# Compressed blocks from sums and differences of chunks, and prompt scores as two stacked float32r products

## The chip, the cores and the metric

The kernel runs on 1 core of one Trainium2 chip. The metric is the device time of one execution in microseconds (us), the median of the runs. Engines: PE (TensorE), DVE (VectorE), ACT (ScalarE), POOL (GpSimd), SP (SyncE, which issues DMAs here). Each runs its own program in order; they wait for each other through semaphores.

## The reference

One decoder layer for a prompt of 1024 tokens and 8 sample sequences of one new token over a paged cache of 2048. What matters here is one part of the sparse attention:

```
compress(rows, pos_emb, w1, w2):            # keys and values, 2 groups, head dim 64
    block n = rows 16 n .. 16 n + 31        # 32 rows, next block 16 rows on: two neighbours share a chunk of 16
    blk = (rows[block] + pos_emb).reshape(nb, groups, 32 * 64)
    return gelu(blk @ w1) @ w2              # w1: 2048 x 256, w2: 256 x 64
s = q . k / 8  over compressed keys, selected keys (top blocks) and the last 512 keys
p = masked softmax(s);  o = p . v  for each of the three, then gated and added
```

A block's product is `chunk c @ A + chunk c+1 @ B`, where A and B are the two halves of w1. The prompt has 63 blocks, each sample sequence 127. The prompt needs scores for 8 tiles of 128 tokens, 8 heads and three branches, with up to 1024 keys; all of it is f32, with a softmax behind it. Queries, keys and state are kept in f32; big weight products are done as three float32r products of a rounded part and a rest.

## The kernel before, in words

`build` runs stages one after the other, each a block with a program per engine; all engines meet between blocks.

`stage_project` (twice, to 458 us) normalises, projects and rotates; it leaves the turned (transposed) queries `qT` and keys `kselT`, `kwinT` in SBUF.

`stage_sequences` (458.7 to 940 us) compresses nine sequences (0 is the prompt, 1 to 8 the samples) and does the samples' attention. Its loop has eleven steps. Step s compresses the keys of sequence s (`compress(s, 0)`), then does the value product of sequence s-2 (`values`), the scores of s-1 (`scores`), and compresses the values of s (`compress(s, 1)`), with the block importance of s-1 between its quarters. The order is written by hand for each engine. In a `compress`, PE transposes the cached rows in four groups (L998, `turn_rows(0..3)`, two PSUM banks in turn), ACT copies each to `XT` (L1148, `keep_turned`), and PE multiplies: four quarters, each 4 row tiles of w1 by two halves of the 256 columns, 8 products with 254 moving columns (127 blocks, 2 groups; 126 for the prompt) in plain f32 (L1017). An f32 product shows as two MATMUL records. ACT applies the GELU straight from PSUM (L1157), and `compressed(q)` (L1035, L1040) multiplies by w2 at the start of the next keys' compress, before its first quarter. Under it, DVE copies turned keys (L1274), takes maxima (L1308, L1339), scales (L1289, L1292) and ranks the 30 blocks of a sequence by comparing all with all (L1327 to L1335); ACT copies scores (L1188) and does the exps (L1169, L1174, L1193). GELU and exp need different tables, each load shows as ACT_TABLE_LOAD. At the start of this stage DVE also gates the prompt's retention output (L1224 to L1233) and does the samples' retention step (L1238 to L1255), and PE computes the position bias (L957).

`stage_attention` (940.3 to 1310 us) goes through 192 units: 8 query tiles, 4 heads per group, 2 groups, 3 branches. For each unit: scores (L1471) with a mask added as a bf16 product (L1474), DVE maximum (L1567, L1570), ACT exp (L1517), PE transposes (L1488), copies by DVE or ACT (L1576, L1532), value products (L1500). A query has zeros in the other group's 64 partitions (`qz`, made by POOL in `pad_queries`), so that one f32 product with keys of both groups gives one group's scores; scores run three units ahead. Keys and queries lie in SBUF from the stages before; SP only loads `w_out`.

`stage_mix_out` and `stage_feed_forward` (to the end) multiply by w_out and do the SwiGLU; L374, L379 and L383 are the float32r product, rounding and rest, which all stages share.

## Time and profile before

| | |
|---|---|
| median of 3 runs | 2213.86 us (2211.0 to 2223.89) |
| the profiled execution | 2213.31 us, its span 2211.6 |
| PE, weight loads, DVE, ACT, POOL busy | 2095.4, 1812.5, 772.1, 599.4, 459.7 us |
| mean granted TensorE clock | 0.974 |
| L1017 (compress) | 1152 records |
| L1471 (prompt scores) | 720 records |
| L374 (float32r products) | 5184 and 1512 records |

In the rows below, a group of instructions is named by its line in the kernel, engine, operation, what it writes and reads, the shape, and the count. PE is the matmul, PEld the weight load that overlaps it. Brackets at the end of a row give how long the engine had been idle before it and what released it. A merged row of time covers all its instructions from the first start to the last end; the end of a matmul lies some 0.2 us after the next may start. The names arena, core, kept, halves, hidden are SBUF tensors, banks is PSUM.

### The profile page before, as it was taken

The page shows a single profiled execution, that of the slowest core. Times are in us where ns is not written, and L with a number is a line of the kernel's source. Part 1 is how long each engine was busy: PE and PEld are TensorE (multiplying, and loading weights), DVE is VectorE, ACT ScalarE, POOL GpSimd, SP SyncE. Part 2 cuts the span into 40 slices and gives each one's busy share as a digit, 9 for nine tenths or more (in the row PEclk, how much of TensorE's full clock was granted, in tenths as well). Part 3 has the DMA queues.
Part 4 walks back from the last instruction along what each step waited for, and adds up shares of the span by engine and source line. Part 5 has one row for each costly group of instructions (what it writes and reads, how often), then busy time and mean ns, then how long its engine had stood idle before and what let it go on. Part 6 is the DMA issues. An engine that isn't in the chain of part 4 may idle for free. (4 is left out here: it accounts for less than half of the span.)

```text
span 2211.6 us, 34591 instructions
## 1 busy us (share of the span) xinstructions
PE 2095.4 (95%) x12669; PEld 1812.5 (82%) x12669; DVE 772.1 (35%) x1454; ACT 599.4 (27%) x1269; POOL 459.7 (21%) x433
## 2 busy tenths in 40 slices
PE   6999989978999999699999989899999999999998
PEld 5777768856776777488888868699999999999987
DVE  5544433554344444455444453301111011111015
ACT  4310112112333333265444442222110111111112
POOL 0111112212223321210000002133321333223330
PEclk9999989988999999699999989999999999999999
DMA  5211102047886773020000002121111111111123
GB/s 176 68 58 39 39 26 84 30 103 123 112 108 103 100 100 52 24 68 1 1 1 1 1 29 106 66 75 43 45 48 47 48 47 43 43 51 44 45 69 116
DMA packets 159455, 131.89 MB, mean 60 GB/s; under 512 B 15257, under 2 KB 147050, under 8 KB 159010
## 3 DMA queue, kind: packets, MB, share of 16 engines
q1 hardware_dynamic: 155234, 121.85, 23.7%
q0 software_dynamic: 4096, 8.40, 2.2%
q8 instruction: 76, 1.25, 0.2%
q14 instruction: 49, 0.40, 0.1%
HBM read 117.85 MB, written 16.55 MB: 61 GB/s over the span
## 5 line engine op out<-in xcount | busy, mean ns | idle before, releaser
L374 PE MATMUL banks<-halves 128*128 128x344 f32 (+4 forms) x5184 | 855.8, 327 | 12.6 <-POOL halves L383 12.6
L374 PEld LDWEIGHTS banks<-halves 128*128 128x128 f32 (+1 forms) x5184 | 821.2, 188 | 43.1 <-issue 7.5
L383 POOL TENSOR_TENSOR halves<-core,halves 128x1024 fp32r<-128x1024 f32 (+1 forms) x143 | 243.8, 1712 | 641.4 <-ACT halves L379 491.4
L374 PE MATMUL banks<-hidden 128*128 128x512 f32 (+3 forms) x1512 | 349.7, 387 | 9.1 <-DVE hidden L383 9.1
L374 PEld LDWEIGHTS banks<-hidden 128*128 128x128 f32 (+1 forms) x1512 | 254.7, 179 | 77.6 <-issue 9.7
L1017 PE MATMUL banks<-arena 128*128 128x254 f32 (+1 forms) x1152 | 248.4, 372 | 11.2 <-ACT arena L1148 7.1
L1017 PEld LDWEIGHTS banks<-arena 128*128 128x128 f32 x1152 | 208.8, 194 | 37.4 <-issue 6.2
L379 ACT ACTIVATE halves<-core 128x1024 fp32r<-128x1024 f32 (+1 forms) x85 | 88.1, 1047 | 388.4 <-PE banks L374 369.6
L1929 DVE TENSOR_TENSOR core<-banks,core 128x344 f32<-128x344 f32 x66 | 34.0, 516 | 440.6 <-PE banks L374 440.6
L1500 PE MATMUL banks<-kept,arena 128*128 128x64 f32 (+1 forms) x1184 | 172.9, 277 | 6.4 <-ACT arena L1532 4.2
L1500 PEld LDWEIGHTS banks<-kept,arena 128*128 128x128 f32 (+1 forms) x1184 | 151.1, 191 | 20.6 <-issue 16.9
L1471 PE MATMUL banks<-kept,arena 128*128 128x128 f32 (+4 forms) x720 | 161.2, 342 | 0.9 <-PEq L849 0.9
L1517 ACT ACTIVATE arena<-banks,arena 128x63 f32<-128x63 f32 (+8 forms) x192 | 109.5, 571 | 166.9 <-DVE arena L1570 149.7
L1570 DVE TENSOR_REDUCE arena<-banks 128x1 f32<-128x640 f32 (+4 forms) x184 | 102.4, 558 | 128.1 <-PE banks L1474 126.4
L1471 PEld LDWEIGHTS banks<-kept,arena 128*128 128x128 f32 x720 | 116.6, 192 | 32.6 <-issue 16.2
L930 POOL DMA_DIRECT2D arena<-in_cache_kv x128 | 67.8, 530 | 235.4 <-PE banks L1058 209.7
L1488 PE MATMUL banks<-core,arena 128*128 128x128 f32 (+1 forms) x592 | 109.7, 280 | 0.2 <-ACT arena L1517 0.2
L561 POOL TENSOR_TENSOR retention<-core,retention 128x256 f32<-128x256 f32 (+1 forms) x36 | 30.3, 841 | 261.4 <-ACT core L544 261.4
L1576 DVE COPY arena<-banks 63x128 f32<-63x128 f32 (+4 forms) x129 | 59.5, 461 | 62.3 <-PE banks L1488 61.2
L1148 ACT ACTIVATE arena<-banks 128x512 f32<-128x512 f32 (+1 forms) x72 | 39.7, 577 | 147.5 <-PE banks L998 147.0
L629 DVE TENSOR_TENSOR retention<-core,retention 128x128 f32<-128x128 f32 (+1 forms) x72 | 37.6, 564 | 119.9 <-ACT core L544 119.9
L1880 ACT ACTIVATE core<-banks 128x344 f32<-128x344 f32 x66 | 30.2, 458 | 175.1 <-PE banks L374 175.0
(203 smaller groups left out, 1791.2 us busy)
## 6 DMA issues: line engine op xcount, KB each, us to landing
core<-in_cache_kv SPq DMA_DIRECT2D x128, 128.0 KB, 5.5
core<-in_w_gate SPq DMA_DIRECT2D x22, 512.0 KB, 3.8
core<-in_w_up SPq DMA_DIRECT2D x22, 512.0 KB, 3.7
core<-in_x_prompt SPq DMA_DIRECT2D x16, 512.0 KB, 3.4
arena<-in_cache_kv SPq DMA_DIRECT2D x128, 64.0 KB, 5.1
arena<-in_cache_kv POOLq DMA_DIRECT2D x128, 64.0 KB, 3.9
retention<-in_w_in SPq DMA_DIRECT2D x16, 448.0 KB, 6.2
...
```

Of the source, the lines that this page charges most:

```text
L374: done = pe.matmul(out, left[a], right[b], start=(first and i == 0), stop=(last and i == 2))
L379: return act.activation(hi, x, ACT.Copy)
L383: return engine.tensor_tensor(lo, x, hi.bitcast(F32), ALU.subtract)
L930: pool.dma_start(m.selv[16 * at:16 * at + 16, half, :, :], io.pool[bass.ds(page[pg], 1), :, :, 384:512].rearrange("a c t n -> (a c) t n")) ...
L1017: last = pe.matmul(m.banks[:, 2 + mt, 0:2 * nb], m.w1[kv][:, k, P * mt:P * mt + P], m.XT[:, k % 8, :, k // 8:k // 8 + nb], start=(k == 0), ...
L1148: act.activation(m.XT.rearrange("p (h j) g c -> p j h g c", h=2)[:, i, :, :, 0:nch], m.banks[:, u % 2, :].rearrange("p (g c h) -> p h g c" ...
L1471: last = pe.matmul(out[:, lo:hi], m.qz[t % 2][:, hh, g, :], keys[:, lo:hi], start=True, stop=not mask)
L1488: last = pe.transpose(m.banks[0:w, 5 + i % 2, P * x:P * x + P], m.prob[u % 4][:, P * (first + x):P * (first + x) + w], m.ident)
L1500: last = pe.matmul(m.banks[:, 7, HD * (u % 8):HD * (u % 8) + HD], m.pts[i % 3][0:w, P * x:P * x + P], v[0:w, 64 * g:64 * g + 64], start=(f ...
L1517: act.activation(m.prob[i % 4][:, 0:width(i)], scores_of(i, width(i)), ACT.Exp, bias=m.nmax[:, i % 8:i % 8 + 1], accum_out=m.sums[UNITS[i] ...
L1570: dve.tensor_reduce(peak, out, AX.X, ALU.max, negate=True).then_inc(s["c_max"], 1)
L1576: dve.tensor_copy(m.pts[i % 3][0:w, 0:P * n], m.banks[0:w, 5 + i % 2, 0:P * n]).then_inc(s["c_kept_dve"], 1)
```

## The change

- Compress: `m.odd` holds the odd chunks, `before` = even - odd of the same pair, `behind` = odd - next even. With A + B summed once per sequence set (`w1sum`), three products serve two neighbouring blocks: A on `before`, A + B on `odd`, B on `behind`. The block that starts at an even chunk is the first plus the second, the one that starts at an odd chunk is the second less the third. A quarter has 12 products of 128 moving columns (64 for the prompt) in place of 8 of 254. ACT copies only the odd chunks, DVE makes the differences out of PSUM and SBUF (`split`), ACT copies the shared product to SBUF (`keep_shared`), DVE forms the hidden rows (`summed`), and the GELU reads them from SBUF. `compressed` moves behind the first quarter. The pair `A + B` is added by DVE (keys) and POOL (values).
- The prompt's and samples' retention steps on DVE move in between the splits, sums and steps. Before, they came first.
- Blocks now stand in the order even, odd; masks and importance sums follow.
- Prompt scores: the stationary operand is the rounded part of a query tile on partitions 0 to 63 and its rest on 64 to 127, the moving one a group's keys, rounded, on both halves, and then their rest on both halves: two float32r products in place of one f32 product.
- For that, the project stage stores turned keys and queries to DRAM and waits for it; the sequences stage loads the keys at its end; the attention stage loads queries tile by tile, ACT rounds, POOL (queries) and DVE (keys) subtract, at its start and then a tile ahead. The bf16 masks are made in the sequences stage and kept.
- Semaphores of the project stage are cleared and freed behind it, with a barrier of all engines; SBUF is laid out anew.

The core of it:

```diff
+            def store_queries(t):
+                sp.dma_start(io.turned_queries[:, :, t * P:(t + 1) * P].rearrange("h p t -> p h t"),
+                             m.qT[:, :, t * P:(t + 1) * P]).then_inc(s["turned_out"], 16)
...
+                if ch in (5, 6) and t == 2:
+                    sp.wait_ge(s["tkept"], turns_before(n))
+                    sp.dma_start(io.turned_keys[ch - 5], (m.kselT, m.kwinT)[ch - 5]).then_inc(s["turned_out"], 16)
+                if kind == "q" and t >= 2:
+                    sp.wait_ge(s["tkept"], turns_before(n - 1))
+                    store_queries(t - 2)
...
+                sp.wait_ge(s["turned_out"], 16 * (2 + TP))
...
-                if kv == 0 and q:
-                    compressed(q - 1)
-                done = 2 * q + kv
-                if q == 0 and kv:
-                    pe.wait_ge(s["b_w_in1"], 48)
-                wait(pe, "b_gelu", 2 * done)
+                done, mc = 2 * q + kv, nch // 2
+                wait(pe, "b_summed", done)
                 for i in range(4):
                     if i in (1, 2):
                         turn_rows(i + 1)
-                    if done == 0 and i % 2 == 0:
-                        pe.wait_ge(s["b_w_in0" if i else "b_w_first"], 96 if i else 64)
-                    pe.wait_ge(s["b_kept_act"], kept_by(TURN_AT["kv"[kv], q, i] + 1, False))
-                    for k in (i, 4 + i, 8 + i, 12 + i):
+                    if q == 0 and (i == 0 or kv == 0 and i == 2):
+                        pe.wait_ge(s["b_w_sum"], 3 if kv else i // 2 + 1)
+                    pe.wait_ge(s["b_split"], kept_by(TURN_AT["kv"[kv], q, i] + 1, False))
+                    for j in (i, 4 + i):
                         for mt in range(2):
-                            last = pe.matmul(m.banks[:, 2 + mt, 0:2 * nb], m.w1[kv][:, k, P * mt:P * mt + P],
-                                             m.XT[:, k % 8, :, k // 8:k // 8 + nb], start=(k == 0), stop=(k == 15))
+                            for part, (w, x) in enumerate(((m.w1[kv][:, j, :], m.before), (m.w1sum[kv][:, j, :], m.odd),
+                                                           (m.w1[kv][:, 8 + j, :], m.behind))):
+                                bank, at = (3, P * mt) if part == 2 else (2, 256 * part + P * mt)
+                                out = m.banks[:, bank, at:at + P].rearrange("p (g c) -> p g c", g=2)[:, :, 0:mc]
+                                last = pe.matmul(out, w[:, P * mt:P * mt + P], x[:, j, :, 0:mc],
+                                                 start=(j == 0 and mt == 0 and part != 1), stop=(j == 7),
+                                                 skip_group_check=True)
+                    if i == 0 and kv == 0 and q:
+                        compressed(q - 1)
...
-                    act.activation(m.XT.rearrange("p (h j) g c -> p j h g c", h=2)[:, i, :, :, 0:nch],
-                                   m.banks[:, u % 2, :].rearrange("p (g c h) -> p h g c", g=2, h=2)[:, :, :, 0:nch],
-                                   ACT.Copy).then_inc(s["b_kept_act"], 1)
+                    act.activation(m.odd.rearrange("p (h j) g c -> p j h g c", h=2)[:, i, :, :, 0:mc],
+                                   turned_chunks(u, 1)[:, :, :, 0:mc], ACT.Copy).then_inc(s["b_kept_act"], 1)
+
+            def keep_shared(q, kv):
+                act.wait_ge(s["b_hidden"], 2 * q + kv + 1)
+                act.activation(products(m.shared, q), products(m.banks[:, 2, 256:512], q), ACT.Copy
+                               ).then_inc(s["b_shared"], 1)
...
+                act.wait_ge(s["b_summed"], 2 * q + kv + 1)
...
+                    keep_shared(step, 0)
...
+                    keep_shared(q, 1)
+                    if q + 1 in SEQS_B:
+                        keep_turned(q + 1, 0, range(2))
                     gelu(q, 1)
                     if q + 1 in SEQS_B:
-                        keep_turned(q + 1, 0)
+                        keep_turned(q + 1, 0, range(2, 4))
...
+            def split(q, kv, parts=range(4)):
+
+                mc = chunks_of(q) // 2
+                for i in parts:
+                    u = TURN_AT["kv"[kv], q, i]
+                    odd, before, behind = (x.rearrange("p (h j) g c -> p j h g c", h=2)[:, i, :, :, 0:mc]
+                                           for x in (m.odd, m.before, m.behind))
+                    even = turned_chunks(u, 0)[:, :, :, 0:mc]
+                    dve.wait_ge(s["b_kept_act"], kept_by(u + 1, False))
+                    dve.tensor_tensor(before, even, odd, ALU.subtract)
+                    dve.tensor_tensor(behind[:, :, :, 0:mc - 1], odd[:, :, :, 0:mc - 1], even[:, :, :, 1:mc], ALU.subtract
+                                      ).then_inc(s["b_split"], 1)
+
+            def summed(q, kv):
+
+                dve.wait_ge(s["b_shared"], 2 * q + kv + 1)
+                wait(dve, "b_gelu", 2 * (2 * q + kv))
+                shared = products(m.shared, q)
+                dve.tensor_tensor(products(m.hidden[:, 0, :], q), products(m.banks[:, 2, 0:256], q), shared, ALU.add)
+                dve.tensor_tensor(products(m.hidden[:, 1, :], q), shared, products(m.banks[:, 3, 0:256], q), ALU.subtract
+                                  ).then_inc(s["b_summed"], 1)
...
+            split(0, 0, range(2, 4))
+            norm_sums(0)
+            summed(0, 0)
+            split(0, 1)
+            norm_sums(1)
+            summed(0, 1)
+            split(1, 0, range(2))
+            norm_sums(2)
+            norm_sums(3)
+            split(1, 0, range(2, 4))
+            sample_out()
+            summed(1, 0)
+            split(1, 1)
+            sample_state()
+            summed(1, 1)
+            split(2, 0, range(2))
+            norm_gate(1, 1)
+            norm_gate(2, 2)
             dve.wait_ge(s["r_state_out"], 16)
...
                     dve.tensor_scalar(SR[:, WINC], SR[:, WINC], bst[:, 7:8], None, ALU.mult)
+                    if step in SEQS_B:
+                        split(step, 0, range(2, 4))
                     dve.wait_ge(s["b_sel_exp"], q)
                     inverse(bst[:, 6:7], m.gs[0:8, q - 1, 1:2], bst[:, 8:9])
                     dve.tensor_scalar(SR[:, SEL], SR[:, SEL], bst[:, 8:9], None, ALU.mult).then_inc(s["b_scaled"], 1)
+                    if step in SEQS_B:
+                        summed(step, 0)
...
                 q = step - 1
+                if step == 2:
+                    split(2, 0, range(2, 4))
+                    summed(2, 0)
...
                     dve.tensor_reduce(bst[:, 3:4], SR[:, WINC], AX.X, ALU.max, negate=True).then_inc(s["b_win_max"], 1)
+                    if step in SEQS_B:
+                        split(step, 1, range(2))
...
+                    if step in SEQS_B:
+                        split(step, 1, range(2, 3))
...
                     own.after(dve.tensor_tensor(cg, cg, ce, ALU.add))
+                    if step in SEQS_B:
+                        split(step, 1, range(3, 4))
                     own.after(dve.tensor_reduce(imp, cg, AX.X, ALU.add))
...
                     own.after(added)
+                    if step in SEQS_B:
+                        summed(step, 1)
+                    if step + 1 in SEQS_B:
+                        split(step + 1, 0, range(2))
                     dve.tensor_reduce(bst[:, 5:6], SR[:, SEL], AX.X, ALU.max, negate=True).then_inc(s["b_sel_max"], 1)
+                if step in (3, 4):
+                    norm_gate((0, 3)[step - 3], step)
...
+            def load_queries(t):
+
+                for g in range(2):
+                    src = io.turned_queries[:, HD * g:HD * g + HD, P * t:P * t + P].rearrange("h d t -> d h t")
+                    for half in range(2):
+                        sp.dma_start(m.qstage[t % 2][HD * half:HD * half + HD, g, :, :], src
+                                     ).then_inc(s[f"c_q_in{t % 2}"], 16)
+
+            for t in range(2):
+                load_queries(t)
...
+            sp.wait_ge(s["c_keys_lo"], 4)
...
-                        last = pe.matmul(out[:, lo:hi], m.qz[t % 2][:, hh, g, :], keys[:, lo:hi], start=True, stop=not mask)
+                        for v in range(2):
+                            last = pe.matmul(out[:, lo:hi], m.qs[t % 2][:, g, hh, :], pair[v][:, first + lo:first + hi],
+                                             start=(v == 0), stop=(v == 1 and not mask))
...
+            def queries_hi(t):
+
+                act.wait_ge(s[f"c_q_in{t % 2}"], 64 * (t // 2 + 1))
+                wait(act, "c_scores", PER_TILE * (t - 1))
+                round_to_hi(act, m.qs[t % 2], m.qstage[t % 2]).then_inc(s["c_q_hi"], 1)
+
+            queries_hi(0)
+            act.wait_ge(s["c_keys_in"], 128)
+            for g in range(2):
+                for what in range(2):
+                    round_to_hi(act, m.keys[what][g][0], m.kstage[what][g]).then_inc(s["c_keys_hi"], 1)
+            queries_hi(1)
...
+            def queries_lo(t):
+
+                pool.wait_ge(s["c_q_hi"], t + 1)
+                low = slice(HD, P)
+                rest_to_lo(pool, m.qs[t % 2][low], m.qstage[t % 2][low], m.qs[t % 2][low]).then_inc(s["c_queries"], 1)
+
+            queries_lo(0)
+            pool.wait_ge(s["c_queries"], 1)
+            queries_lo(1)
+            for t in range(TP - 1):
+                if t:
+                    pool.wait_ge(s["c_weighted"], t)
+                    queries_lo(t + 1)
+                pool.wait_ge(s["c_queries"], t + 2)
...
+            for g in range(2):
+                for what in range(2):
+                    dve.wait_ge(s["c_keys_hi"], 2 * g + what + 1)
+                    rest_to_lo(dve, m.keys[what][g][1], m.kstage[what][g], m.keys[what][g][0]).then_inc(s["c_keys_lo"], 1)
...
+            s.retire(PROJECT_ONLY)
```

## Rows read from the trace of the kernel before

**Rows 1.** Busy time of each engine in stretches: stretch, length, then busy (instructions).

```profile
618.00:666.00 48.00, 46.67 (x270) 36.26 (x268) 21.21 (x34) 17.61 (x31) 11.92 (x17) 1.00 0.73 103
...
1000.00:1100.00 100.00, 98.52 (x745) 85.06 (x744) 48.30 (x95) 50.55 (x150) 7.97 (x6) 1.00 0.01 1
```

**Rows 2.** Groups of PE by shape: prompt scores. Count, then busy us and mean ns.

```profile
L1471 PE MATMUL banks<-kept,arena 128*128 128x128 f32 x368 | 67.5, 276 | 0.0
L1471 PE MATMUL banks<-kept,arena 128*128 128x384 f32 x112 | 47.1, 502 | 0.0
...
L1471 PE MATMUL banks<-kept,arena 128*128 128x512 f32 x64 | 32.8, 594 | 0.0
...
L1471 PE MATMUL banks<-kept,arena 128*128 128x256 f32 x48 | 14.3, 380 | 0.0
```

**Rows 3.** Order of time, PE, sequences stage: start, length, line, shape, count.

```profile
471.25 3.73 PE L1017 MATMUL banks<-arena 128*128 128x126 f32 x32
...
718.46 1.09 PE L998 MATMUL banks<-core,arena 128*128 128x128 f32 x8
719.95 3.67 PE L1017 MATMUL banks<-arena 128*128 128x254 f32 x16 [0.40 <-ACT arena L1148]
...
724.73 0.38 PE L1100 MATMUL banks<-core,arena 8*8 8x127 f32 x2 [0.96 <-DVE core L1311]
...
753.91 1.47 PE L1049 MATMUL banks<-core,arena 8*128 8x8 f32 x21 [0.22 <-DVE arena L1292]
```

**Rows 4.** Order of time, PE, float32r at 512 and 256 columns, and the attention.

```profile
435.56 5.82 PE L374 MATMUL banks<-hidden 128*128 128x512 f32 x24
...
1182.10 1.00 PE L1500 MATMUL banks<-kept,arena 128*128 128x64 f32 x8
...
1183.94 1.68 PE L1471 MATMUL banks<-kept,arena 128*128 128x512 f32 x6
...
2157.89 5.20 PE L374 MATMUL banks<-halves 128*128 128x256 f32 x42
```

**Rows 5.** Weight loads of float32r (L374) and bf16 (L1474): ns min/median/max.

```profile
L374 PEld LDWEIGHTS banks<-halves x5184: 87/188/338, 1321.1 to 2197.2; 128*128 128x128 f32 x198, 128*8 128x8 f32 x2
...
L1474 PEld LDWEIGHTS banks<-arena x224: 100/100/154, 940.6 to 1302.3; 128*128 128x128 bf16 x112
```

**Rows 6.** Order of time, DVE: end of project, a step, start of attention.

```profile
456.56 0.67 DVE L652 TENSOR_SCALAR kept<-banks 128x512 f32<-128x512 f32 x1
...
734.44 2.27 DVE L1339 TENSOR_REDUCE core<-arena 8x1 f32<-8x2049 f32 x1
...
750.59 0.48 DVE L1289 TENSOR_SCALAR arena<-arena,core 8x512 f32<-8x512 f32 x1
...
940.93 0.22 DVE L1567 TENSOR_REDUCE arena<-banks 128x1 f32<-128x63 f32 x1 [0.95 <-PE banks L1474]
```

**Rows 7.** DMA issues of the page: KB each, us from issue to landing.

```profile
core<-in_w_gate SPq DMA_DIRECT2D x22, 512.0 KB, 3.8
```

**Rows 8.** Groups of DVE and ACT by shape: count, busy us, mean ns.

```profile
L663 DVE COPY retention<-banks 128x256 f32<-128x256 f32 x32 | 13.5, 423 | 5.4 <-PE banks L763 5.1
...
L379 ACT ACTIVATE halves<-core 128x1024 fp32r<-128x1024 f32 x84 | 87.9, 1056 | 388.4 <-PE banks L374 369.6 <-DMA core<-in_w_down 16.5 <-DMA core<-in_w_out 1.4
```

**Rows 9.** Order of time, ACT: the copy of a keys half's last transposes.

```profile
746.87 0.60 ACT L1148 ACTIVATE arena<-banks 128x512 f32<-128x512 f32 x1 [3.27 <-PE banks L998]
```

**Rows 10.** Order of time, PE: gaps and what follows them.

```profile
508.49 1.94 PE L998 MATMUL banks<-core,arena 128*128 128x128 f32 x8 [7.58 <-issue]
...
531.21 5.25 PE L1017 MATMUL banks<-arena 128*128 128x254 f32 x16 [2.62 <-ACT arena L1148]
...
564.72 1.03 PE L1071 MATMUL banks<-core,arena 128*128 128x128 f32 x8
...
891.68 2.41 PE L1049 MATMUL banks<-core,arena 8*128 8x8 f32 x21 [6.33 <-DVE arena L1292]
```

**Rows 11.** Busy time of each engine over the samples' retention step on DVE.

```profile
514.20:538.40 24.20, 21.58 (x103) 18.69 (x103) 23.80 (x13) 6.73 (x12) 5.84 (x1) 0.93 0.59 73
```

263 lines of the change are left out of this document (165 added, 98 removed).

## The prediction

> **What bounds the kernel now.** I read the windows by stage first [rows 1]. In a step of the sample sequences (618 to 666 us) the PE is busy 46.67 of 48 us, and in the attention of the prompt (1000 to 1100 us) 98.52 of 100, at a granted clock of 1.00; DVE and ACT are busy about half of the time or less. So the end is set by the stream of PE records, and a change pays only if it shortens that stream without making the PE wait for DVE or ACT. Then I read the PE groups by shape [rows 2] for the counts, and the order of time on each engine for pitches and for what each is late for. Mean durations don't serve, since records overlap: a pitch is the merged time less one lone record (0.27 to 0.38), over the count less one.
>
> All sums are against the profiled execution, 2213.3 us (span 2211.6), 0.6 under the median of the runs.
>
> **Pitches.** A plain f32 product is two records. At 254 columns 16 records take 3.67 us, 0.219 each; at 126 columns 32 take 3.73, 0.112 each [rows 3]: half the columns, half the time. At 64 columns eight take 1.00, 0.103 each [rows 4], so there the load of 128 weight columns sets the pace. For 128 columns I take 0.112. Scores in f32: 512, 256 and 128 columns, two records each, take 1.68 us [rows 4], so 0.84 ns a column: 0.431, 0.324, 0.216, 0.108 a record for 512, 384, 256, 128. A float32r product is one record, 0.237 at 512 columns (24 in 5.82) and 0.120 at 256 (42 in 5.20) [rows 4].
>
> **Prompt scores, in float32r.** The count of records stays: one product of two becomes two of one. From the counts in [rows 2], 64 records of 512 columns save 0.194 each, 12.4 us; 112 of 384 save 0.145 (the value between), 16.2; 48 of 256 save 0.096, 4.6. The 368 of 128 columns, and the compressed ones of 63, save nothing, being at the pace of the weight load. Sum 33.2 us, all on the PE's path. Bounds: 29 (a tenth lost to waits, since DVE's and ACT's part of a unit is unchanged) to 59 (rival D).
> By the Trainium skill, "TensorE: Matmul & The Clock Gate", the section on weight-path perf modes, a weight of 128 columns that is not FP32 is read in four parallel chunks. If float32r counts as not FP32, narrow score products get cheaper too, which is rival D. The trace speaks against it: a float32r LDWEIGHTS lasts 188 ns in the median, a bf16 one 100 [rows 5].
>
> **Start of the prompt stage.** Before, DVE's first maximum comes at 940.93 [rows 6], 0.6 after the stage begins. After, queries come back from DRAM: four loads issued over some 1.5 us, the last landing 3.8 later [rows 7]; then ACT rounds one query tile and four key tiles (5 x 1.06 [rows 8]) and DVE subtracts the last (about 1.1), all ahead of that maximum: 940.3 + 1.5 + 3.8 + 5.3 + 1.1 = 952.0. With a colder PE I take +11.5 (8 to 14). Later query tiles are loaded, rounded and subtracted a tile ahead of use: nothing.
>
> **Compressed blocks, the PE's share.** A quarter had 16 records of 254 columns and gets 24 of 128: 3.50 to 2.69 us. Over a step's eight quarters that is 6.5 us less. For sequence 0 it is a loss: 64 records at 0.112 become 96 at about 0.105, 2.9 more for keys and for values.
>
> **Compressed blocks, the chain.** What feeds a quarter was one ACT copy (0.60 for 512 columns [rows 9]). Now it is an ACT copy of 256 (0.39) and two DVE subtractions of 256 (0.42 each [rows 8], 0.75 for two that overlap a little), and where DVE does them is fixed by its program. I follow one cycle, from the values half of a step through the keys half of the next, 718.46 to 753.91 before [rows 3], with t = 0 at 718.46.
> - Quarter one started at 1.5 on ACT's copy; a split stands behind it now: 2.2 to 4.9. The importance product waits for ACT and DVE, 6.3 before [rows 3], less 0.4 of shorter copies: 5.9. Transposes 0.4, quarter two to 9.3, transposes, quarter three to 12.5.
> - DVE has 9.7 us of work from the importance product to the maximum of the selected scores (724.73 to 734.44 [rows 3, 6]). Two splits (1.5) and a wait for ACT's copy (0.3) go in between: 17.4. Split four is ready at 13.1, so quarter four ends at 15.8 and the next transposes at 16.7.
> - The sums out of PSUM (`summed`, 0.75) stand behind the ranking: 18.15; then the first split of the next keys: 18.9. **The PE waits 2.2 us**, where it waited for no DVE before.
> - Quarter 18.9 to 21.6, `compressed` 1.5, transposes, quarter two, transposes: 26.7.
> - `split(step, 0, range(2, 4))` stands on DVE behind the scaling of the window scores, their exp stands on ACT behind the copy of the last transposes, three small copies and a table load. In the trace this goes from 746.87 [rows 9] to 751.07, the end of that scaling [rows 6]: 4.2 us, less 0.2 for the shorter copy. So 26.85 + 4.0 + 0.75 = 31.6. **The PE waits 4.9 us** with nothing else to do.
> - Quarters three and four: 37.0, against 35.45 before; the rest of the cycle (13.8) is as it was.
> So a cycle of 49.2 gets 1.6 longer although the PE has 6.5 less to do; I take 1.8, for the cycles in which POOL's copies slow DVE. And gaps cost clock: after a gap of 2.62 us 16 records took 5.25 instead of 3.67 [rows 10, 3], and after one of 6.33 the next group 2.41 instead of 1.47, so part of it ran at the lower of the clock's levels (1.2, not 2.4 GHz). I take 1.6 once a cycle; 0 to 3.2 is possible. There are six such cycles, with the keys of steps 3 to 8: 6 x 3.4 = +20.4 (10 to 31). After step 8's values the PE waits for the maximum of the selected scores (6.33 [rows 10]), which comes 2.3 later, by two splits and the sums: +2.3.
>
> **Boundary and start of the sequences stage.** DVE's last copy of queries ends at 457.2 [rows 6]; their store must land before the stage ends, 3.8 later by the nearest row [rows 7]: 461.0 instead of 458.4. With issue and the new barrier 0.8 more: +3.4 (1.5 to 6). The sample retention moves in between the splits. Sequence 1's keys start at 508.49 [rows 10], when its pages are grouped; +3.4 and two more small loads in SP's queue, 1.1: 513.0. Transposes, copy and split 2.3, quarters 10.8, `compressed` 1.5, transposes 0.9: 528.5. DVE's retention was one piece of 24.2 us [rows 11], some 13.6 up to the sum of squares, which is `sample_out`: from 524.5 (after split four) to 538.1; sums and split 539.6. The PE waits 10, and runs the four quarters, the first cold, until 553.6. `sample_state`, the other 10.5, from 549.8: 560.3, sums and split 561.8, another 7 of waiting. A cold quarter 4.7, `compressed` 1.5, three quarters and transposes 9: 577.0, against 564.72 [rows 10]. That is +12.3, of which 3.4 is the boundary: +8.9 (4 to 14). Sequence 0's loss of 5.8 lies in front of the page wait (7.58 of idle PE [rows 10]), which hides it; without that wait it would count.
>
> **Sum.** 2213.3 + 3.4 + 8.9 + 20.4 + 2.3 + 11.5 - 33.2 = 2226.6. Feed-forward, output product and projections keep their work: 0.
>
> **Rivals.** A measurement of this kernel can tell about 0.5% (11 us) from no change.
> A (forecast): as above, 2227. Chance 0.40.
> B, the other side: **DVE keeps up**: quarter three is not held by the exp chain, nor the sums by the ranking. It decides at a PE wait under 0.5 us a cycle. Then the six cycles give -39 and the last nothing: 2213.3 + 3.4 + 8.9 - 39.0 + 11.5 - 33.2 = 2165. For it: DVE is busy only 21 of 48 us [rows 1]. Against: it is the order that makes the wait, not the load. Half true, it gives some 2195. Chance 0.20 for 2165 to 2202.
> C: the gaps are there but the clock holds, 6 x 1.8 in place of 6 x 3.4: 2217. For it: the gaps are short. Against: the row after 2.62 us. Chance 0.18.
> D: narrow float32r weights load fast. A 128-column record then costs half of a 256-column one and a fixed part, 0.066 in place of 0.112: 368 x 0.045, and with the compressed ones 26 us: 2201. Chance 0.07.
> E: both gaps of a cycle cost 1.6: 6 x 5.0: 2236; with the start at its upper bound 2245. Chance 0.15.
>
> The likeliest's own range is 2213 to 2240; 8 in 10 of all cases lie in 2188 to 2246. Under 2202.8 us: B and D, 0.27. Over 2224.9: E and seven tenths of A, 0.43. Between: 0.30.
>
> **What would show it.** Quarters of 24 records at 0.112. A PE gap of about 5 us before quarter three of each key half from step 3 on, ended by a DVE subtraction, and one of about 2 before quarter one; a cycle of 51 to 53 us. The prompt stage shorter by 22 us net, its first maximum 11 later than before, counted from the stage's start. If the gap before quarter three is missing, the chain through the window exp is wrong and B holds; if 128-column score records follow each other under 0.09 apart, D.

## The result, and the profile after

The changed kernel takes 2308.57 us (median of 4 runs, 2302.55 to 2309.52) against 2214.28 (4 runs): 1.0423 of the time before, 95% interval 1.0406 to 1.0440. The forecast was 2227 (2188 to 2246). The side was right, the size was not: +94 us where +13 was forecast. The profiled execution has a span of 2307.4 us and a mean granted clock of 0.929; before, 2211.6 and 0.974. One execution of e9 below, 2588.9 us at a granted clock of 0.743, is left out of its ratio.

From the page of the changed kernel, busy time of each engine over the span:

```profile
PE 2101.8 (91%) x13245; PEld 1876.2 (81%) x13245; DVE 851.8 (37%) x1645; ACT 607.1 (26%) x1299; POOL 465.2 (20%) x425
```

PE does 6 us more by this row, though many of its products got cheaper. The windows by stage say why. Columns as in [rows 1]; the number behind POOL's is the granted clock, 1.00 being 2.4 GHz ("warm" below) and 0.50 being 1.2 ("cold"):

```profile
471.00:491.00 20.00, 20.00 (x96) 20.00 (x96) 8.54 (x8) 0.56 (x2) 4.53 (x1) 0.50 0.50 116
...
504.00:524.00 20.00, 20.00 (x97) 20.00 (x96) 4.45 (x6) 0.56 (x2) 3.79 (x2) 0.50 0.86 160
...
1028.00:1131.00 103.00, 97.58 (x476) 92.28 (x477) 41.81 (x108) 44.00 (x158) 13.43 (x6) 0.50 0.21 52
...
1068.00:1108.00 40.00, 40.00 (x196) 38.15 (x196) 12.85 (x33) 15.39 (x56) 4.16 (x2) 0.50 0.05 14
...
1148.00:1188.00 40.00, 39.97 (x338) 38.50 (x338) 21.44 (x43) 23.56 (x70) 5.13 (x2) 1.00 0.05 15
```

Three stretches run at the lower level while PE is busy nearly all the time: the products of sequence 0's keys, those of its values (between them the products of the position bias bring the clock up, and a wait of 2.44 us follows), and the first 103 us of the prompt's attention. PE gets through 476 records in those 103 us and 338 in a later 40, so at the later rate the same records would need 56 us: less a wait of 4.42, some 42 us are lost there (the mix of shapes differs, so this is an estimate from those two rows). Before, the first 103 us of this stage had a mean granted clock of 0.98.

PE in order of time, changed kernel: start, length, line (L1065 the products of the compressed blocks, L1046 and L1125 transposes, L1103 and L1112 the values half, L1154 importance, L1635 scores of the prompt, L1653 its transposes, L1647 the last transposes of the mix), shape, count, idle time before and its releaser:

```profile
463.21 1.12 PE L1046 MATMUL banks<-core,arena 128*128 128x128 f32 x4 [4.76 <-POOL arena L990]
470.29 5.36 PE L1065 MATMUL banks<-arena 128*128 128x64 f32 x24 [5.96 <-DVE arena L1306]
...
534.31 1.09 PE L1046 MATMUL banks<-core,arena 128*128 128x128 f32 x8 [0.26 <-ACT arena L1181]
...
563.56 5.27 PE L1065 MATMUL banks<-arena 128*128 128x128 f32 x24 [12.89 <-DVE arena L1306]
...
585.05 4.79 PE L1065 MATMUL banks<-arena 128*128 128x128 f32 x24 [6.43 <-DVE arena L1306]
...
607.21 1.97 PE L1125 MATMUL banks<-core,arena 128*128 128x128 f32 x8 [6.82 <-DMA core<-out]
...
731.16 2.92 PE L1065 MATMUL banks<-arena 128*128 128x128 f32 x24 [1.11 <-DVE arena L1306]
...
743.93 2.94 PE L1065 MATMUL banks<-arena 128*128 128x128 f32 x24 [2.24 <-DVE arena L1306]
749.04 2.92 PE L1065 MATMUL banks<-arena 128*128 128x128 f32 x24 [1.29 <-DVE arena L1306]
...
761.94 7.78 PE L1065 MATMUL banks<-arena 128*128 128x128 f32 x48 [4.80 <-DVE arena L1306]
769.65 1.47 PE L1103 MATMUL banks<-core,arena 8*128 8x8 f32 x21
...
973.52 2.40 PE L1103 MATMUL banks<-core,arena 8*128 8x8 f32 x21 [6.34 <-DVE arena L1422]
...
1019.01 0.23 PE L1118 MATMUL banks<-core,arena 8*128 8x8 f32 x1 [0.37 <-DVE arena L1431]
1028.27 0.60 PE L1635 MATMUL banks<-kept_pairs,pairs 128*128 128x64 f32 x2 [9.03 <-POOL pairs L404]
...
1035.69 0.42 PE L1653 MATMUL banks<-core,softmax 128*64 128x128 f32 x1 [4.42 <-ACT softmax L1697]
...
1410.72 1.09 PE L1647 MATMUL banks<-core,softmax 128*128 128x128 f32 x4 [4.59 <-DVE softmax L1791]
```

Set against the same places of before ([rows 3, 10], and the first score and last mix at 940.46 and 1314.51), the 95.8 us of the span come from:

| stretch | before | after | more | forecast |
|---|---|---|---|---|
| up to the first transposes of the sequences | 459.76 | 463.21 | +3.5 | +3.4 |
| from there to sequence 1's scores | 104.96 | 144.00 | +39.0 | +8.9 |
| to the last transposing of probabilities | 326.96 | 366.31 | +39.4 | +22.7 |
| to the last product of the sequences | 47.92 | 45.72 | -2.2 | 0 |
| PE's wait for the first prompt score | 0.86 | 9.03 | +8.2 | } +11.5 |
| the prompt's attention | 374.05 | 382.45 | +8.4 | } -33.2 |
| the rest | 897.1 | 896.7 | -0.4 | 0 |

Within the prompt's attention each tile's mix is transposed once, so the starts of these transposes cut the stage into the same pieces of work in every trace. From the first score on, us:

| trace | first two pieces | third | other five |
|---|---|---|---|
| before | 57.7 | 37.2 | 279.1 |
| changed kernel | 98.6 | 35.3 | 248.6 |
| e3, f32 scores, hole in front | 70.3 | 37.2 | 279.2 |
| e2, f32 scores, the change's gaps | 76.2 | 37.2 | 279.1 |
| e1, float32r scores, gaps filled | 78.3 | 33.1 | 250.1 |
| e9, gaps filled, f32 scores in the first two tiles | 59.7 | 33.1 | 248.5 |

So the changed kernel gained 32.5 us on the score products in its last six pieces, and lost 40.9 in the first two.

### The profile page after: what moved, and what is told of

It is laid out like the page before. It is cut to its first block and busy times, and to the rows that moved or that the text cites. A ratio compares the mean times of both kernels' runs of the same rounds, so it can differ in the third digit from the quotient of the medians.

```text
span 2307.4 us, 36086 instructions
## 1 busy us (share of the span) xinstructions
PE 2101.8 (91%) x13245; PEld 1876.2 (81%) x13245; DVE 851.8 (37%) x1645; ACT 607.1 (26%) x1299; POOL 465.2 (20%) x425
## 5 line engine op out<-in xcount | busy, mean ns | idle before, releaser
L395 PE MATMUL banks<-halves 128*128 128x344 f32 (+4 forms) x5184 | 854.9, 327 | 13.1 <-POOL halves L404 13.1
L1065 PE MATMUL banks<-arena 128*128 128x128 f32 (+1 forms) x1728 | 245.8, 310 | 88.6 <-DVE arena L1306 88.6
L1065 PEld LDWEIGHTS banks<-arena 128*128 128x128 f32 x1728 | 238.3, 224 | 95.2 <-DVE arena L1306 44.0
L1665 PE MATMUL banks<-kept,softmax 128*128 128x64 f32 (+1 forms) x1184 | 191.3, 297 | 6.1 <-ACT softmax L1712 4.3
L1665 PEld LDWEIGHTS banks<-kept,softmax 128*128 128x128 f32 (+1 forms) x1184 | 169.6, 211 | 15.9 <-issue 8.4
L1697 ACT ACTIVATE softmax<-banks,softmax 128x64 f32<-128x64 f32 (+8 forms) x192 | 109.4, 571 | 144.4 <-DVE softmax L1762 135.6
L1762 DVE TENSOR_REDUCE softmax<-banks 128x1 f32<-128x640 f32 (+4 forms) x184 | 102.4, 558 | 116.1 <-PE banks L1639 115.3
L1653 PE MATMUL banks<-core,softmax 128*128 128x128 f32 (+1 forms) x592 | 120.6, 301 | 4.4 <-ACT softmax L1697 4.4
L1635 PE MATMUL banks<-pairs 128*128 128x128 f32 (+3 forms) x592 | 123.0, 338 | 0.7 <-DVE pairs L404 0.7
L1635 PEld LDWEIGHTS banks<-pairs 128*128 128x128 f32 x592 | 105.8, 222 | 3.6 <-issue 1.0
L1653 PEld LDWEIGHTS banks<-core,softmax 128*128 128x128 f32 (+1 forms) x592 | 80.3, 167 | 9.3 <-ACT softmax L1697 4.6
L1768 DVE COPY softmax<-banks 64x128 f32<-64x128 f32 (+4 forms) x129 | 59.4, 460 | 75.3 <-PE banks L1653 74.8
```

The source lines that it names most:

```text
L395: done = pe.matmul(out, left[a], right[b], start=(first and i == 0), stop=(last and i == 2))
L1065: last = pe.matmul(out, w[:, P * mt:P * mt + P], x[:, j, :, 0:mc], start=(j == 0 and mt == 0 and part != 1), stop=(j == 7), skip_group_che ...
L1635: last = pe.matmul(out[:, lo:hi], m.qs[t % 2][:, g, hh, :], pair[v][:, first + lo:first + hi], start=(v == 0), stop=(v == 1 and not mask))
L1653: last = pe.transpose(m.banks[0:w, 5 + i % 2, P * x:P * x + P], m.prob[u % 4][:, P * (first + x):P * (first + x) + w], m.ident)
L1665: last = pe.matmul(m.banks[:, 7, HD * (u % 8):HD * (u % 8) + HD], m.pts[i % 3][0:w, P * x:P * x + P], v[0:w, 64 * g:64 * g + 64], start=(f ...
L1697: act.activation(m.prob[i % 4][:, 0:width(i)], scores_of(i, width(i)), ACT.Exp, bias=m.nmax[:, i % 8:i % 8 + 1], accum_out=m.sums[UNITS[i] ...
```

## The experiments

Ratios are to the kernel before, run on the same chip; us in brackets are medians. A gain over the changed kernel is the difference of two medians taken on different chips; from the ratios it comes out 1 to 3 us smaller. Line numbers in rows of an experiment are those of its own kernel.

**e1. The prompt stage's gaps filled.** On PE, ahead of the first score and behind the third:

```diff
+FILL_A, FILL_B = 10, 5
...
+            def fill(count):
+                for _ in range(count):
+                    pe.matmul(m.banks[:, 6, :], m.ident, m.vsel[:, 0:4, :], start=True, stop=True)
+
+            fill(FILL_A)
...
+                if x == AHEAD:
+                    fill(FILL_B)
```

> The changed kernel, with 10 extra 128x512 f32 products of resident data in front of the prompt attention's first score product and 5 more behind its third unit, into a bank that nothing has read from yet: PE has no idle 9.03 and 4.42 us there any more. Theory (the gap lets the clock fall to the 1.2 GHz level, and the small float32r, transposing and value products behind it don't bring it up for 100 us; once up, they hold it): the stretch 1028 to 1131 us runs at the granted clock 1.00 from its start, which is worth about 103 us x (1 - 196/338 records in equal 40 us slices) = 43 us: 2308 - 43 = 2265, at least 2255 to 2275. Rival (the mix of small products cannot hold the high level for the first two tiles, whatever stands in front): the clock falls again within some 20 us of the first score, and the time stays at 2300 to 2310. Rival 2 (the start is set by the waits on the queries and key parts, not by the clock): 2305 to 2312.

Measured 1.0346, 1.0329 to 1.0364 (2289.57): 19 us gained, between the two forecasts. Windows of its trace, with the wait at which the clock fell:

```profile
1028.00:1048.00 20.00, 18.15 (x124) 13.63 (x123) 15.22 (x40) 12.40 (x51) 3.59 (x2) 1.00 0.58 151
...
1060.17 0.98 PE L1673 MATMUL banks<-kept,softmax 128*128 128x64 f32 x4 [1.13 <-DVE softmax L1776]
...
1059.00:1062.00 3.00, 1.87 (x12) 1.86 (x11) 2.19 (x6) 1.30 (x5) 1.16 (x1) 0.71 0.06 16
1062.00:1100.00 38.00, 38.00 (x187) 36.38 (x187) 11.77 (x32) 15.30 (x52) 1.29 (x1) 0.50 0.05 13
```

The stage starts at 1.00 now, and loses it after some 30 us, right behind a wait of 1.13 us at the end of the first tile; it stays low for 41 us, PE busy throughout. The kernel before has the same wait and the same fall, and is back within 4 us:

```profile
966.35 0.63 PE L1500 MATMUL banks<-kept,arena 128*128 128x64 f32 x4 [0.99 <-DVE arena L1576]
...
968.00:971.00 3.00, 3.00 (x14) 2.54 (x14) 0.43 (x1) 0.75 (x3) 0.00 (x0) 0.50 0.00 0
971.00:974.00 3.00, 3.00 (x29) 2.89 (x26) 1.52 (x5) 2.14 (x9) 0.00 (x0) 0.95 0.00 0
```

So neither theory holds alone. At this place, behind a wait of 1.0 to 1.6 us, the clock falls with either kind of score product (before, e1, e9, e11 and e12; not in e6). How long it stays down differs: 41 us here, with float32r scores behind it, and under 4 in the other four, with f32 ones.

**e2. The same gaps, f32 scores.**

```diff
-                        for v in range(2):
-                            last = pe.matmul(out[:, lo:hi], m.qs[t % 2][:, g, hh, :], pair[v][:, first + lo:first + hi],
-                                             start=(v == 0), stop=(v == 1 and not mask))
+                        last = pe.matmul(out[:, lo:hi], m.qs[t % 2][:, g, hh, :].bitcast(F32),
+                                         pair[0][:, first + lo:first + hi].bitcast(F32), start=True, stop=not mask)
```

> The changed kernel, with each prompt score product done once, as plain f32 on the rounded part of the keys, in place of two float32r products; the low part of the keys drops out of the scores. All staging, waits and the two gaps at the stage's start stay. Theory (it is the two cheap float32r products that leave the array too little to do for the clock to rise): the clock comes back to 1.00 within some 20 us of the stage's start, as the kernel before had it from 945 us on, and the stage costs about what it did before, 374 us, plus the two gaps: 1.0 to 1.05 of the kernel before's, 2308 - 10 = 2298 give or take 6, with the low-clock stretch gone. Rival (a stage that starts cold stays cold for 100 us whatever its score products are): the low clock lasts as long, the f32 products are dearer, and the time is 2320 to 2350.

Measured 1.0477, 1.0459 to 1.0494 (2318.55). Windows of its trace:

```profile
1028.00:1048.00 20.00, 14.93 (x70) 12.55 (x70) 12.29 (x28) 8.88 (x34) 3.10 (x1) 0.50 0.62 156
1048.00:1068.00 20.00, 20.00 (x97) 17.77 (x96) 7.22 (x28) 8.91 (x39) 0.00 (x0) 0.50 0.29 56
1068.00:1088.00 20.00, 19.61 (x163) 17.82 (x162) 10.62 (x28) 12.72 (x47) 5.12 (x2) 0.96 0.10 27
```

The low stretch is 40 us, not 103: with f32 scores the clock comes back 60 us sooner, behind the same two gaps (9.14 and 4.33 here). The time is still 10 us above the changed kernel, since the wide scores cost their old price again (33 us by the forecast's count). My 2298 reckoned with a return within 20 us.

**e3. The kernel before, with a hole** ahead of the first prompt score.

```diff
             pe.wait_ge(s["c_masks"], 4)
+            pe.wait_ge(s["hole"], 1)
...
             own = Links(dve, s, "own_dve")
+            for _ in range(7):
+                own.after(dve.tensor_tensor(m.prob[3], m.vsel.rearrange("p t n -> p (t n)"),
+                                            m.vwin.rearrange("p t n -> p (t n)"), ALU.add))
+            dve.tensor_tensor(m.prob[3], m.vsel.rearrange("p t n -> p (t n)"), m.vwin.rearrange("p t n -> p (t n)"),
+                              ALU.add).then_inc(s["hole"], 1)
```

> The kernel before, with its first prompt score product held back by eight 128x1024 additions on DVE of about 1.1 us each, so that PE idles about 9 us where it idled 0.86 us. Theory A (f32 products bring the clock back soon): 2214 + 8 to 9 for the hole + up to 10 for a cold start = 2222 to 2233. Rival (any hole there costs a long stretch at the 1.2 GHz level): 2214 + 9 + about 40 = 2255 to 2270. If both this and the f32 scores in the changed kernel come out short, the hole is only half of the cause and the lighter products the other half.

Measured 1.0107, 1.009 to 1.0124 (2236.16), 22.5 us more, 3 above the range of theory A and far from the rival. PE's first score, and windows of its trace:

```profile
950.40 0.66 PE L1472 MATMUL banks<-kept,arena 128*128 128x63 f32 x2 [10.86 <-DVE arena L1562]
```

```profile
950.00:960.00 10.00, 9.60 (x47) 8.54 (x48) 4.10 (x17) 4.55 (x21) 0.00 (x0) 0.50 0.49 170
...
970.00:990.00 20.00, 19.77 (x114) 17.57 (x112) 9.18 (x28) 9.13 (x37) 3.99 (x3) 0.63 0.01 1
990.00:1010.00 20.00, 19.39 (x166) 17.84 (x167) 9.63 (x29) 12.54 (x48) 1.22 (x2) 1.00 0.00 1
```

10.0 us are the hole (10.86 less 0.86), 12 to 13 the cold stretch of some 35 us behind it. So a hole there costs its length and as much again with f32 scores. With the float32r ones the cold stretch costs some 42 us by the rates above, and 37 set against the same pieces of e9 (41.1 more in the first three, less the wait of 4.42).

**e4. Sequence 0 over 128 columns**, the upper half zeros.

```diff
-                done, mc = 2 * q + kv, nch // 2
+                done, mc = 2 * q + kv, 64
...
+            for x in (m.odd, m.before):
+                own.after(dve.memset(x[:, :, :, 32:64], 0.0))
```

> The changed kernel, with sequence 0's compressing products taken over 128 columns in place of 64 (the other 64 are zeros from a memset and their results are not read). The products count stays at 384 records. At the high clock a 128-column record took 0.115 us and at the low one 0.22; a 64-column one was seen at 0.22 only. Theory (narrow products, limited by the weight load, leave the array idle enough that the clock stays at the 1.2 GHz level): the clock rises within the first 10 us, sequence 0 takes about 2 x (4 x 2.8 + a few) us less, sequence 1's keys start 15 to 22 us earlier, 2287 to 2295. Rival (the clock stays low there because PE comes cold out of the gap before it, whatever the width): 2306 to 2312, with 0.22 us a record still. Rival 2 (the 64-column record costs 0.22 at either clock): the clock may rise in the wide run, which then also saves, so the other run of narrow products behind a fill has to tell it.

Measured 1.0354, 1.0337 to 1.0371 (2291.81): 17 us gained by doing twice the columns. PE of its trace, both halves of sequence 0:

```profile
469.13 4.37 PE L1065 MATMUL banks<-arena 128*128 128x128 f32 x24 [5.97 <-DVE arena L1306]
473.55 2.84 PE L1065 MATMUL banks<-arena 128*128 128x128 f32 x24
...
493.10 4.33 PE L1065 MATMUL banks<-arena 128*128 128x128 f32 x24 [2.44 <-DVE arena L1306]
```

Out of the same gaps, the clock is up within the first quarter of 24 records.

**e8. Sequence 0 with 64 columns, the gap ahead of it filled.**

```diff
                 turn_rows(1)
+                if q == 0 and kv == 0:
+                    for _ in range(7):
+                        pe.matmul(m.banks[:, 7, :], m.ident, m.vsel[:, 0:4, :], start=True, stop=True)
```

> The changed kernel, with seven 128x512 f32 products of resident data in PE's 5.96 us wait ahead of sequence 0's first compressing product; the compressing products keep their 64 columns. Theory (64-column products cannot hold the high clock): if the clock is up at their start it falls again within 10 to 15 us, most records cost 0.22 us still and the time is 2300 to 2309. Rival 1 (it was the cold start alone; once up, 64-column products hold the clock): 0.11 us a record, sequence 1 starts some 20 us earlier, 2286 to 2293 as with 128 columns. Rival 2 (a 64-column record costs 0.22 at the high clock too): the windows show a granted clock near 1.00 with 0.22 us a record.

Measured 1.04, 1.0379 to 1.0421 (2300.3). PE of its trace, keys and then values of sequence 0:

```profile
471.65 2.79 PE L1068 MATMUL banks<-arena 128*128 128x64 f32 x24
...
493.94 5.29 PE L1068 MATMUL banks<-arena 128*128 128x64 f32 x24 [2.44 <-DVE arena L1309]
499.45 5.22 PE L1068 MATMUL banks<-arena 128*128 128x64 f32 x24
504.89 10.34 PE L1068 MATMUL banks<-arena 128*128 128x64 f32 x48
```

It split in two. Entered at the high clock, a 64-column record costs 0.116 us and the level holds for that half. Behind the bias products and a 2.44 us gap, the same products ran 21 us at 0.22 without bringing it back; e4's, behind the same gap, did. So here they kept a clock they found, for 11 us, and did not raise it in 21. Rival 2 (0.22 at either clock) is out.

**e5. The float32r scores alone**, compressing and retention as before. Of the change, all of `stage_attention`, the stores and loads of queries and keys and `kcbP` stay; in `stage_sequences` the products are again:

```diff
-                    for j in (i, 4 + i):
+                    for k in (i, 4 + i, 8 + i, 12 + i):
...
+                            last = pe.matmul(m.banks[:, 2 + mt, 0:2 * nb], m.w1[kv][:, k, P * mt:P * mt + P],
+                                             m.XT[:, k % 8, :, k // 8:k // 8 + nb], start=(k == 0), stop=(k == 15))
```

> One half of the change alone: the two stacked float32r score products with all their staging (queries and keys out to DRAM and back, rounded and low parts), while the compressing keeps the four products, the copies and the retention work of the kernel before. Theory (the clock is the cost of this half): +3.4 for the boundary, +12.6 for the two gaps at the prompt stage's start, -39 for the score products at the high clock, +43 for the 100 us at the 1.2 GHz level = 2214 + 20 = 2234, 2228 to 2242; so this half alone is slower, and the sequences' part of the loss (some 75 us) belongs to the compressing. Rival (the scores pay, all of the loss is in the sequences): 2185 to 2200. Rival 2 (the staging of keys also delays the sequences, for instance the transfer that scores of sequence 1 waited for): 2250 or more.

Measured 1.0075, 1.0047 to 1.0104 (2228.92), as expected. Its sequences end at 941.7, 2.1 later than before (rival 2 is out); its attention takes 16 us more, with the same low stretch as the changed kernel:

```profile
951.00:1051.00 100.00, 94.85 (x463) 89.53 (x463) 40.79 (x106) 42.91 (x156) 13.31 (x5) 0.50 0.21 53
```

So of the 94 us some 17 belong to the scores and 77 to the compressing (1.0423 less 1.0075, of 2214).

**e6. e5, start filled, f32 products in the first two tiles, the rounding of keys spread.**

```diff
+                        if t < PLAIN and br:
+                            last = pe.matmul(out[:, lo:hi], m.qs[t % 2][:, g, hh, :].bitcast(F32),
+                                             m.kstage[br - 1][g][:, first + lo:first + hi], start=True, stop=not mask)
+                        for v in range(0 if t < PLAIN and br else 2):
```

> The same half, with three edits in the prompt stage: ten extra 128x512 f32 products of resident data fill PE's wait for the queries; in the first two query tiles the score products of the two long branches are one f32 product on the staged keys (as many records as the two float32r ones where the piece is 128 columns wide, but four passes each); the rounding of the keys is spread over those two tiles. Theory (a filled start plus products heavy enough hold the high clock until the wide pieces begin): granted clock 1.00 from the stage's start but for moments, 2214 + 3.4 + 9 (the wait for the queries stays) - 35 = 2191, 2186 to 2200. Rival (the rest of the mix, transposes and 64-column value products, still lets the clock fall in tile 1 or 2 for 40 us or more, as it did behind the fill alone): 2208 to 2225.

Measured 1.0072, 1.0052 to 1.0092 (2225.2), short of the forecast; its six times lie at two levels, 2206.5 and 2208.0 (the profiled one) and 2224.6 to 2228.0. The trace shows 1.00 through the first two tiles, as hoped, and then a hole of my own making. PE, and ACT ahead of it:

```profile
1017.73 1.51 PE L1583 MATMUL banks<-kept,softmax 128*128 128x64 f32 x6 [13.63 <-ACT softmax L1630]
```

```profile
1015.58 1.06 ACT L398 ACTIVATE pairs<-softmax 128x1024 fp32r<-128x1024 f32 x1 [13.58 <-DMA softmax<-turned_queries]
```

The staged keys live where the output weights go, so I had held those loads back until the scores of the first two tiles were done; the queries from the fourth tile on then queued behind them on SP. The two shorter executions have a mean granted clock of 0.970 and 0.971, the other four 0.961 or 0.962. An estimate from these is that the four spent some 40 us more at the lower level, which fits the 18 us. What put them there no trace shows.

**e9. e6, with all query loads ahead of the weights' on SP's queue** (and without e6's wait for two tiles' scores). Against the changed kernel:

```diff
-            sp.wait_ge(s["c_keys_lo"], 4)
-            for k in range(NSLOT):
-                load_w_out(sp, s, m, io, k)
             for t in range(2, TP):
                 sp.wait_ge(s["c_queries"], t - 1)
                 load_queries(t)
+            sp.wait_ge(s["c_keys_lo"], 4)
+            for k in range(NSLOT):
+                load_w_out(sp, s, m, io, k)
```

> The half with the scores alone and its filled start, now with the loads of the output weights behind all loads of queries on SP's queue. In the run before, the queries of the fourth tile were issued behind the weights' loads, ACT waited 13.58 us for them, PE stood 13.63 us, and the clock stayed low for some 15 us behind it. Theory (that hole and its cold stretch are all that is left between this half and its gain): PE goes through at the high clock, 2207 - 13 - 7 = 2187, 2182 to 2193, and the two levels that the run before showed (2207 and 2226) are gone. Rival (the mix of light products loses the clock in another place once the hole is gone): 2200 to 2212.

Measured **0.9898, 0.9881 to 0.9914** (2191.65), within the forecast. It beats both kernels, the one before by 1%. Windows of its trace, with the wait ahead of its one fall of the clock:

```profile
950.00:1000.00 50.00, 45.39 (x365) 39.75 (x364) 28.90 (x89) 33.90 (x131) 8.33 (x4) 0.97 0.11 33
...
980.26 0.63 PE L1580 MATMUL banks<-kept,softmax 128*128 128x64 f32 x4 [1.56 <-DVE softmax L1683]
...
983.00:986.00 3.00, 3.00 (x17) 2.87 (x16) 2.00 (x4) 1.00 (x4) 0.00 (x0) 0.50 0.34 99
987.00:990.00 3.00, 3.00 (x29) 2.84 (x28) 1.40 (x4) 1.88 (x9) 0.00 (x0) 1.00 0.02 5
```

The wait at the end of the first tile is here too (1.56), and the clock falls; with f32 scores in the second tile it is back within 4 us, where e1 took 41.

From the end of its sequences to the output product it takes 357.2 us (941.7 to 1298.84), where before took 381.5 (939.6 to 1321.10). That is 24 less, with the 9 us of fill in it. The last six pieces of the stage take 34.8 us less than before: the 33 us that the forecast had for the products are there.

**e7. The last two differences of the next keys ahead of the window's scaling on DVE.**

```diff
                 if 1 <= q <= NB_SEQ:
+                    if step in SEQS_B:
+                        split(step, 0, range(2, 4))
                     dve.wait_ge(s["b_win_exp"], q)
...
                     dve.tensor_scalar(SR[:, WINC], SR[:, WINC], bst[:, 7:8], None, ALU.mult)
-                    if step in SEQS_B:
-                        split(step, 0, range(2, 4))
```

> The changed kernel, with the last two differences of the next sequence's keys taken before the window's softmax scaling in DVE's order, not behind it, in each of the seven cycles. Theory (PE's 4.80 us in front of the third and fourth quarter is DVE's order, and that gap also costs 2.3 us of clock): the six full cycles fall from 54.5 towards 50 us, 20 to 35 us in all, 2275 to 2288. Rival (the differences come no earlier, because they wait for ACT's copy behind the GELU, and only push the scaling and the transposing of probabilities back): 2303 to 2315.

Measured 1.0329, 1.0307 to 1.0352 (2285.02): 24 us. The cycle is 48.8 to 51.2 us, from 54.3 to 55.2. What it left of waits, in the cycle before 755.98:

```profile
735.91 2.94 PE L1065 MATMUL banks<-arena 128*128 128x128 f32 x24 [2.24 <-DVE arena L1306]
...
748.95 5.52 PE L1065 MATMUL banks<-arena 128*128 128x128 f32 x48
755.98 1.47 PE L1103 MATMUL banks<-core,arena 8*128 8x8 f32 x21 [1.50 <-DVE arena L1422]
```

48 records take 5.52, where they took 7.78 behind the 4.80 us gap (the row at 761.94 above): that gap cost 2.26 of clock on top. A wait of 1.50 for the scaling of the selected scores came up in its place.

**e10. DVE's retention work moved into sequence 0.**

```diff
             norm_sums(0)
+            norm_sums(1)
             summed(0, 0)
             split(0, 1)
-            norm_sums(1)
+            norm_sums(2)
+            norm_sums(3)
+            sample_out()
             summed(0, 1)
-            split(1, 0, range(2))
-            norm_sums(2)
-            norm_sums(3)
-            split(1, 0, range(2, 4))
-            sample_out()
+            split(1, 0)
+            sample_state()
             summed(1, 0)
             split(1, 1)
-            sample_state()
             summed(1, 1)
```

> The changed kernel, with DVE's retention work (the sums of squares, the samples' state) moved ahead into the stretch in which DVE waits for sequence 0's products (15 of 65 us busy there), so that sequence 1's differences stand behind less. Theory (the 12.89 and 6.43 us gaps of sequence 1 and the 6.82 us wait for its key pages are the order on DVE, and each also costs a cold start of 2.4 us): sequence 1's scores start 20 to 28 us earlier, 2281 to 2290. Rival (DVE's work only moves, the retention's inputs land too late for it, and the gap comes up in sequence 0): 2300 to 2312.

Measured 1.0338, 1.0315 to 1.0361 (2288.24): 20 us. The waits of 12.89 and 6.43 are 8.73 and 1.14, the one for pages (6.82) is gone, and sequence 1's scores start at 588.03, 19.2 earlier. On SP's queue the store of the new state stands ahead of those pages' loads; in the changed kernel it is issued at 583.61, here at 555.28.

**e11. All repairs together** (e4, e7, e10 and the prompt stage of e9).

> The changed kernel with all repairs together: 128 columns for sequence 0, the differences ahead of the window's scaling, the retention's DVE work early, and the prompt stage with the filled start, f32 products in the first two tiles and the queries' loads first. Theory (the parts add up): 2308 - 17 - 23 - 23 - 38 = 2207, 2198 to 2222: level with the kernel before, and about 20 us above the half with the scores alone, because the cycles still take 50.4 us against 49.2. Rival (the repairs of the sequences overlap, one gap under another): 2225 to 2245.

Measured 1.0028, 1.0013 to 1.0044 (2219.39), inside the range and 12 above the sum. One repair takes from another: with sequence 0 done sooner, PE meets the retention work earlier:

```profile
533.39 4.95 PE L1065 MATMUL banks<-arena 128*128 128x128 f32 x24 [15.32 <-DVE arena L1306]
```

**e12. e11 without three of the ranking's four operations.**

```diff
-                    own.after(dve.tensor_tensor(ce, other, mine, ALU.is_equal))
-                    own.after(dve.tensor_tensor(ce, ce, m.tie[0:8], ALU.mult))
-                    own.after(dve.tensor_tensor(cg, cg, ce, ALU.add))
```

> The version with all repairs, with three of the ranking's four 8x900 operations left out on DVE (equal, times the order, and their sum: so two blocks of the same weight would no longer be told apart by their order), 1.08 + 2.79 + 1.08 us in a cycle. The products, copies and differences stay. Theory (what still keeps a cycle with three products at 50.4 us is the order of work on DVE: PE waits 1.11, 0.69, 2.24, 1.29 and 1.50 us in it, 6.8 us, as much as the fourth product cost): the 2.24 and 1.29 us waits go, the cycle falls to 46.5 to 48 us, and the time by 6 x 3 = 18, to 2196 to 2208. Rival (other engines or transfers are late there as well, ACT's copies and GELU or the pages of values): less than 1 us a cycle, 2212 to 2220.

Measured 0.9927, 0.9907 to 0.9947 (2194.88), 1 us under its range: 24.5 us less than e11, the cycle 47.0 to 47.8. PE in one cycle of its trace:

```profile
696.83 2.84 PE L1065 MATMUL banks<-arena 128*128 128x128 f32 x24
699.94 5.52 PE L1065 MATMUL banks<-arena 128*128 128x128 f32 x48
```

The 2.24 us wait is gone, and for the first time every cycle is under those of before (48.9 to 49.2). It is bought with work left out, so it is a measurement and no version to use; it says that what is left of the loss in the cycle is DVE's work ahead of PE, not the products. One of the operations left out is far longer in the changed kernel than before. The two kernels' traces, before and then changed:

```profile
728.04 1.08 DVE L1329 TENSOR_TENSOR core<-core,arena 8x900 f32<-8x900 f32 x1
...
739.14 1.90 POOL L990 COPY arena<-core 128x2048 f32<-128x2048 f32 x1 [4.36 <-PE banks L1046]
739.19 2.79 DVE L1468 TENSOR_TENSOR core<-core,arena 8x900 f32<-8x900 f32 x1
```

It runs eight times. In five a copy on POOL starts less than 0.5 us ahead of it, and it takes 2.67 to 2.79; in the other three none does, and it takes 1.08, as all eight do before. So the change moved this operation under a copy of POOL. That the copy holds it up is read from this coincidence; no run moved the copy.

## Why the prediction came out as it did

- **Bound by PE's stream, at the high clock**: the premise failed. I read 0.112 and 0.103 us a record off rows at 1.00 [rows 3, 4] and carried them into stretches whose clock the change itself set. This is the step that failed, in two terms: the start of the sequences (30 us of the miss) and the prompt scores (38, with the gaps in front). The other 17 are in the cycles, where the mechanism was right and sizes were off.
- **Start of the sequences, +8.9, measured +39.0.** "96 at about 0.105" for sequence 0: each record took 0.22 (5.22 for 24). Sequence 1's keys start at 534.31 where I had 513.0, and the page wait of 7.58 us hid little of it. e4 gives 17 of it back, and e8 shows that the clock is the cause. The two waits on DVE were sized well: 10 and 7 forecast (the first is 11.1 by my own figures, 528.5 to 539.6), 12.89 and 6.43 measured. The wait for pages behind a late `sample_state` (6.82) I had not seen; e10 took it away. Of the 39.0, 22.4 lie ahead of sequence 1's keys and 16.7 behind (forecast 1.1 and 7.8).
- **Six cycles, 3.4 each, measured 5.1 to 6.3 in five of them and 11.5 in the first.** The +2.3 forecast for the last maximum was 0.0: its wait is 6.34, from 6.33. The chain of the cycle was right: 4.9 and 2.2 us of waiting forecast, 4.80 and 1.29 measured, both ended by DVE's differences. Too small were the clock behind the gap (1.6 against 2.26) and the ranking: quarter four also waits, 2.24 us, since one ranking operation takes 2.79 us and not 1.08; the split four that I had "ready at 13.1" came at 14.9. The 1.11 ahead of quarter one of the values is as forecast (2.2 us after the transposes). In the first cycle PE waits 4.48 and 4.73 us; ahead of the first of these two more of DVE's operations, 0.17 and 2.35 us elsewhere, take 1.92 and 3.98 beside a copy of POOL.
- **Start of the prompt stage, +11.5**: PE waits 8.17 and 4.42 more, so 12.6, inside my 8 to 14. Its chain was a little longer than mine: DVE's four subtractions of keys take 8.08 us in a row, 2.0 each, where I had 1.1 for the last.
- **Prompt scores, -33.2**: right for the products. The changed kernel gained 32.5 us of it in the last six pieces of the stage, e9 34.8. It was eaten up because the stage came cold out of its start and stayed so for 103 us. "With a colder PE" was all that I gave it. This is the other half of the failed step, some 37 to 42 us.
- **Boundary, +3.4**: 3.45.
- **The rivals.** B (DVE keeps up) fell in the changed kernel: e7 got 24 us back by DVE's order alone, e12 another 24.5 by taking work off it. C (the clock holds) is what happened least. D: the float32r weight loads last 187 to 192 ns in the median, as those of [rows 5]. E had the right mechanism in the wrong place: it charged the clock to the gaps of the cycle, not to the stages that start cold. (Its upper figure, 2245, adds up to 2244, and only with the start of the prompt stage at its bound too.)

The Trainium skill, "TensorE: Matmul & The Clock Gate", Part 1, says that what comes before the rise is a matter of time under sustained matmul activity, not of a number of matmuls, and that the ramp is worth under 1% of a typical kernel's span. By that rule 97.58 busy us out of 103 should have brought the clock up near their beginning; the measured row shows 0.50 to the end of it, and the 37 to 42 us lost are nearly 2% of this kernel. The measurement decides: a PE whose records follow each other without a break stayed at the lower level for nearly 100 us here, while in e4 the first 24 products of 128 columns brought it up.

What stays open: why single executions of e6 took 18 us more, and what ends a low stretch. The traces show only where: with float32r scores in the third tile, 24, 24 and 9 us after its first score of 256 columns (changed kernel, e5, e1); with f32 scores in the second, 7 and 5 us after its first score over 256 keys (e2, e3). Whether e9's f32 products would do without the fill was not tried; e1 shows that the fill alone is not enough.

## What to carry to other kernels

A pitch read off a trace holds at its clock only. When a change makes products lighter, narrower or fewer, ask of each stage what stood ahead of it and whether the new stream will bring the clock back: here 33 us of cheaper products were lost again in 103 cold us behind a gap of 9 us, and were worth 24 us, that gap paid, once it was filled and the first tiles kept f32 products. And when work moves to an engine that is half idle, lay it out in that engine's order before counting the gain: a quarter of the products went, and the waits on DVE ate it.
